# Attention softmax read bank by bank: three maxima and three exponentials in place of one of each

## The reference, cut to what matters

```python
def mla_attend(q_n, q_r, k_n, k_r, v):
    s = jnp.einsum('bqhd,bkhd->bhqk', q_n, k_n) + jnp.einsum('bqhr,bkr->bhqk', q_r, k_r)
    p = jax.nn.softmax(s.astype(jnp.float32) * MLA_SCALE, axis=-1)
    return jnp.einsum('bhqk,bkhd->bqhd', p.astype(v.dtype), v)
```

## Time and profile before

| what | value |
|---|---|
| median of three runs (3574.69 to 3577.97) | 3575.5 us |
| the profiled execution, its own time | 3573.7 us |
| its span from the first to the last instruction | 3570.5 us |
| mean granted TensorE clock | 0.938 |
| PE busy in the span | 3135.9 us, 88% |
| DVE busy in the span | 1529.5 us, 43% |
| ACT busy in the span | 1212.9 us, 34% |

### The profile page before, as it was taken

One profiled execution on the slowest core, in us unless ns is written; L12 is line 12 of the kernel. 1 busy time (PEld: TensorE's weight loads), 2 busy tenths in 40 slices (PEclk: granted clock), 3 DMA queues, 4 the chain that ended last, 5 costly groups with the idle time before them and its releaser, 6 DMA issues. The chain is left out here.

```text
span 3570.5 us, 43051 instructions
## 1 busy us (share of the span) xinstructions
PE 3135.9 (88%) x16797; PEld 2670.6 (75%) x16797; DVE 1529.5 (43%) x2588; ACT 1212.9 (34%) x1951; POOL 147.8 (4%) x146
## 2 busy tenths in 40 slices
PE   4538999999999999995995868789999999999598
PEld 4427898889889988983774646668888888887476
DVE  4352454145325523543232121146656665665333
ACT  2321222223222312322212221146666666665310
POOL 0000000000000000000221000000000000000022
PEclk7768999999999999998997989889999999999899
DMA  5401111111111111115333112100010000000332
GB/s 183 159 1 43 30 35 40 46 32 32 45 36 32 32 51 30 32 32 185 95 100 107 38 44 79 62 25 30 28 31 20 26 28 31 21 28 18 124 118 65
DMA packets 214950, 196.06 MB, mean 55 GB/s; under 512 B 9950, under 2 KB 190574, under 8 KB 214770
## 3 DMA queue, kind: packets, MB, share of 16 engines
q1 hardware_dynamic: 197316, 162.62, 14.8%
q0 software_dynamic: 7056, 25.69, 2.0%
q10 hardware_dynamic: 10400, 5.24, 0.5%
HBM read 152.62 MB, written 40.91 MB: 54 GB/s over the span
## 5 line engine op out<-in xcount | busy, mean ns | idle before, releaser
L40 PE MATMUL v_pj<-e_u_hi,v_w_hi 128*128 128x512 f32 (+1 forms) x1728 | 624.5, 361 | 19.3 <-issue 10.3
L41 PE MATMUL v_pj<-e_u_lo,v_w_hi 128*128 128x512 f32 (+1 forms) x1728 | 620.6, 359 | 0.6 <-issue 0.4
L42 PE MATMUL v_pj<-e_u_hi,v_w_lo 128*128 128x512 f32 (+1 forms) x1728 | 620.4, 359 | 0.0
L40 PEld LDWEIGHTS v_pj<-e_u_hi,v_w_hi 128*128 128x128 f32 x1728 | 329.8, 191 | 67.0 <-issue 20.1
L42 PEld LDWEIGHTS v_pj<-e_u_hi,v_w_lo 128*128 128x128 f32 x1728 | 329.3, 191 | 51.8 <-issue 0.7
L41 PEld LDWEIGHTS v_pj<-e_u_lo,v_w_hi 128*128 128x128 f32 x1728 | 329.9, 191 | 47.1
L40 PE MATMUL o_y_bank<-o_w_hi,o_m_hi 128*128 128x512 f32 x576 | 235.9, 410 | 71.9 <-DVE o_w_lo L1095 69.5
L1592 ACT CAST t_pt_hi<-t_ring 128x512 fp32r<-128x512 f32 (+1 forms) x384 | 181.3, 517 | 252.2 <-PE t_ring L1775 252.2
L40 PE MATMUL l_pj<-l_u_hi,l_w_hi 128*128 128x512 f32 (+3 forms) x376 | 160.8, 428 | 81.8 <-DVE l_w_lo L1323 60.7
L41 PE MATMUL o_y_bank<-o_w_lo,o_m_hi 128*128 128x512 f32 x576 | 231.5, 402 | 0.0
L42 PE MATMUL o_y_bank<-o_w_hi,o_m_lo 128*128 128x512 f32 x576 | 231.0, 401 | 0.0
(11 more groups left out here) (327 smaller groups left out, 6219.6 us busy)
## 6 DMA issues: line engine op xcount, KB each, us to landing
v_w_raw<-in_ev_w_in SPq DMA_DIRECT2D x73, 512.0 KB, 3.8
m_w_raw<-in_mod_w SPq DMA_DIRECT2D x24, 1024.0 KB, 5.7
l_w_raw<-in_od_w_in SPq DMA_DIRECT2D x21, 512.0 KB, 4.0
o_m_raw<-mixT SPq DMA_DIRECT2D x20, 512.0 KB, 3.8
mixT<-v_buf SPq DMA_DIRECT2D x16, 512.0 KB, 2.7
o_w_raw<-in_ev_w_out SPq DMA_DIRECT2D x16, 512.0 KB, 3.4
zgT<-l_lat POOLq DMA_DIRECT2D x16, 512.0 KB, 3.1
t_zg<-zgT SPq DMA_DIRECT2D x32, 256.0 KB, 2.7
```

The costliest lines, as they stand in the source:

```text
L40: nc.tensor.matmul(out, whi, xhi, start=first, stop=False)
L41: nc.tensor.matmul(out, whi, xlo, start=False, stop=False)
L42: return nc.tensor.matmul(out, wlo, xhi, start=False, stop=last)
```

## The change

The row's maximum, the exponentials and their sum are now made per bank of `S`. The matmul that finishes a bank increments `qk_done` (three per slot). DVE takes the maximum of each bank as soon as that bank is done, into one column of the new tile `tops`, and then reduces the three columns to the negated maximum in `bias`, after a wait on its own semaphore `top_ok`. ACT makes three exponentials (512, 512 and 256 columns), each with its own sum in a column of `sums` and its own increment of `exp_ok`. PE waits before each bank for the exponential of that bank of the tile before. DVE adds the three sums into `total`, waits for itself (`total_ok`) and takes the reciprocal. The diff:

```diff
+        tops, sums = ([s.sb(f"{n}{x}", [P, 3]) for x in range(2)] for n in ("tops", "sums"))
...
                 act.wait_ge(bias_ok, tile(h, t) + 1)
-                nc.scalar.activation(prob[x][:, :], S[:, 0:T], ACT.Exp, bias=bias[x][:, :], accum_out=total[x][:, :]).then_inc(exp_ok, 1)
+                for j, (k0, n) in enumerate(KEYS):
+                    nc.scalar.activation(prob[x][:, k0:k0 + n], S[:, k0:k0 + n], ACT.Exp, bias=bias[x][:, :],
+                                         accum_out=sums[x][:, j:j + 1]).then_inc(exp_ok, 1)
...
             def maximum(h, t):
-                dve.wait_ge(qk_done, tile(h, t) + 1)
-                nc.vector.tensor_reduce(bias[t % 2][:, :], S[:, 0:T], AX, ALU.max, negate=True).then_inc(bias_ok, 1)
+                for j, (k0, n) in enumerate(KEYS):
+                    dve.wait_ge(qk_done, 3 * tile(h, t) + j + 1)
+                    nc.vector.reduce_max(tops[t % 2][:, j:j + 1], S[:, k0:k0 + n], axis=AX).then_inc(top_ok, 1)
+                dve.wait_ge(top_ok, 3 * tile(h, t) + 3)
+                nc.vector.tensor_reduce(bias[t % 2][:, :], tops[t % 2][:, :], AX, ALU.max, negate=True).then_inc(bias_ok, 1)
 
             def inverse(h, t):
-                dve.wait_ge(exp_ok, tile(h, t) + 1)
+                dve.wait_ge(exp_ok, 3 * tile(h, t) + 3)
+                nc.vector.tensor_reduce(total[t % 2][:, :], sums[t % 2][:, :], AX, ALU.add).then_inc(total_ok, 1)
+                dve.wait_ge(total_ok, tile(h, t) + 1)
                 nc.vector.reciprocal(rec[t % 2][:, :], total[t % 2][:, :]).then_inc(rec_ok, 1)
...
-                if (h, t) != (0, 0):
-                    pe.wait_ge(exp_ok, tile(h, t))
-                for k0, n in KEYS:
+                for j, (k0, n) in enumerate(KEYS):
+                    if (h, t) != (0, 0):
+                        pe.wait_ge(exp_ok, 3 * tile(h, t) - 2 + j)
                     out = S[:, k0:k0 + n]
...
-                    last = nc.tensor.matmul(out, qs[b][:, tok], kr2[1][:, k0:k0 + n], start=False, stop=True)
-                last.then_inc(qk_done, 1)
+                    nc.tensor.matmul(out, qs[b][:, tok], kr2[1][:, k0:k0 + n], start=False, stop=True).then_inc(qk_done, 1)
```

More of the change, by code:

```diff
@@ L1476, in stage_attend @@
         ring_done, ring_hi, ring_free = s.sem("ring_done"), s.sem("ring_hi"), s.sem("ring_free")
-        qk_done, bias_ok, exp_ok, rec_ok, prob_ok = (s.sem(n) for n in ("qk_done", "bias_ok", "exp_ok", "rec_ok", "prob_ok"))
+        qk_done, top_ok, bias_ok, exp_ok, total_ok, rec_ok, prob_ok = (s.sem(n) for n in (
+            "qk_done", "top_ok", "bias_ok", "exp_ok", "total_ok", "rec_ok", "prob_ok"))
         turn_ok, qs_hi_ok, qs_ok = s.sem("turn_ok"), s.sem("qs_hi_ok"), s.sem("qs_ok")
```

## The result

| what | before | changed |
|---|---|---|
| median | 3575.61 us (4 runs) | 3600.03 us (4 runs, 3598.66 to 3603.65) |
| the profiled execution, its own time | 3573.7 us | 3599.6 us |
| its span | 3570.5 us | 3597.7 us |
| mean granted TensorE clock | 0.938 | 0.937 |
| attention: PE's first to last matmul in the span | 2320.5 to 3336.6 | 2321.2 to 3364.6 |

The changed kernel takes 1.0069 times the time before, 95% interval 1.0051 to 1.0086: 24.4 us more, where 26.6 more were forecast. The attention grew from 1016.1 to 1043.4 us, by 27.3, which is the whole difference of the two spans.

A forecast was written before the change was run, and what follows sets the result against it. PE was taken to set the pace, with the ACT-DVE ring full in weight-split slots; 3.90 us per pair times seven, +1.2 (head 14), -1.9 (head 15) gave +26.6, hence 3602 us, range 3583 to 3622.

The forecast's parts named there:

- What bounds the kernel: Attention stretch: PE busy 933 of 964 us sets the pace; the ring of ACT and DVE has no room in split slots.
- the ring of ACT and DVE: Exponential, sum, normalise, cast, low half, next maximum: 5.67 us per qn turn, 6.27 with splits; the change adds 1.06.
- Prices: Costs per turn: three exponentials +0.51 us, join of the sums +0.20, three maxima with their join +0.35.
- E: Start of a tile's (first) exponential; a turn from E to E was forecast at 6.73 us in qn slots, 7.33 with splits.
- Restart: PE restarts on bank 0 0.83 us after E instead of 1.47, saving 0.64 once per run of slots.
- E does not come earlier: Maximum comes 0.84 us sooner when DVE waits for PE, but ACT's casts hold E to within 0.1.
- The sum: Four runs of two turns per head pair: +0.35, +1.51, +1.19, +0.85, together 3.90 us; whole kernel +26.6.
- Rival 1: Faster: ring grows under 0.6 us per turn, the loop through PE stays the bound; 3555 us, chance 0.07.
- Rival 2: No change: joins at 0.06 us, pieces 0.03 cheaper each, ring grows by 0.7; 3575 to 3582 us, chance 0.09.
- Rival 3: Clearly slower: exponential pieces can't overlap reads of the sums, 0.2 to 0.3 us more per turn; about 3617, chance 0.14.
- Rival 4: No release by bank: waits break PE's stream or late exponentials leave no restart gain; 19 us more, 3621, chance 0.04.
- Signs named: Profile signs: last read 1.9 us after E, normalise 2.36, no DVE idle before maxima, PE's waits up, new waits before PV.

## Why the prediction was right, point by point

**What bounds the kernel.** Right. PE sets the pace where it can, the ring of ACT and DVE elsewhere, and the reading that the latter had no room in slots with splits was the one that decided: there the turn grew by 1.01 and the run by 1.36 (15.34 for 13.98).

**Prices.** The exponentials are 0.688, 0.688 and 0.477, taken as 0.69, 0.69 and 0.477 from a line of layer 0. Their starts stand 0.68 and 0.66 apart, so a piece does overlap the read of the sum before it: the condition of the third rival fails. Maxima 0.683 and 0.415 (taken as 0.69 and 0.42), joins 0.156 (taken as 0.16). Every turn came out 0.05 to 0.09 below the forecast. The steps that were off are small: in a qn turn normalise starts 2.34 after E instead of 2.36, and from the first maximum to the next exponential it is 1.84 (2851.75 to 2853.59) instead of 1.84 + 0.04 = 1.88, mostly because the three maxima occupy 1.61 and not 1.64. In a rotation turn 0.07 of the 0.09 lie ahead of the first operation of the rotation (2.55 after E instead of 2.62): the join of the sums, priced there, is hidden behind ACT's cast.

**Restart.** 0.83 after E forecast, 2829.11 to 2829.94 measured, 0.83.

**E does not come earlier.** Nearly right. E of the first tile of a run comes 4.58 after its scores begin (2842.34 to 2846.92) instead of 4.70 (2824.34 to 2829.04). The casts set it now, as forecast. In the kernel before they did not: E followed the end of the maximum (2829.00), and behind the casts alone it could have come 0.11 sooner. That small amount was won in four runs: 0.44 per pair.

**The sum.** Runs: odd to even 14.14 (14.29 forecast), even to odd 15.34 (15.49), rotations 16.65 (16.85), v to PV 19.51 (19.60). Together 3.31 per pair instead of 3.90, less 0.44 for E, 2.87 in all. Head 15 gained 2.25 instead of 1.9.

**What was missed.** The clock. By the terms alone seven pairs would have come to 20 us and the total to about 19. The trace has 27.3; the 1.58 in six odd heads, 9.5 us, brings the sum to 28, within 1 of it. So the forecast of 26.6 stands so close to the result partly because two misses cancel: turns taken 0.05 to 0.09 too long and an effect not thought of. The step at fault is the one that costs PE's wait in t = 5 of an odd head at its own length alone.

**Rivals.** Rival 1 (ring grows by under 0.6) fell: it grew by 1.0. Its premise was sound, as the version with the ring relieved shows: where the ring is not the later one, the release pays (3553.89, near the 3555 worked out for this rival, though with DVE's work in another order). Rival 2 needed joins of 0.06. Rival 3 fell with the starts 0.68 apart. Rival 4 fell: without the release by bank the kernel is 29 to 32 us slower still. Its price of 0.64 in four runs per pair was one run too many, since the run with v does not end in scores.

**Signs named.** Last read 1.93 after E (2848.62 + 0.23), forecast 1.9; normalise 2.34, forecast 2.36; no idle of DVE between the low half and the maxima; PE's waits up from 63.0 to 84.3; waits of up to 0.7 before the eight PV of even heads. PE's two new waits inside a slot cost nothing that a row shows.

## What to carry to other kernels

Before work is split up so that one engine can restart sooner, find the ring that does not pass through this engine and add up one turn of it, with every small operation and hand-over: 0.38 us of joins per turn, on an engine idle for over half of the time, carried some 21 of the 24 us of the loss. Two changes that each fit into the same slack don't fit together, so costs found one at a time can't be added. And when the ring is the bound, first move work out of it (here behind the next tile's maxima), since only then does the early release pay: alone the two edits cost 24 and 10 us, together they gained 22.

## What the runs showed of the hardware that was not expected

**A single wait can halve the clock behind it.** In the attention PE is busy nearly without a break, and yet the granted clock fell to 1.2 GHz around the restart behind one wait in t = 5 of an odd head, at the earliest 0.2 us before it and at the latest 1.5 us after it, each time for 3.41 us. Over the kernels run, by PE's idle time there:

| kernel | idle before the restart, us | odd heads in which the clock fell |
|---|---|---|
| relieved ring (both versions) | none | 0 of 7 and 0 of 7 |
| before, with the low halves moved | 0.43 | 0 of 7 |
| kn twice (two runs) | 0.8 | 0 of 7 and 0 of 7 |
| before | 1.43 | 0 of 7 |
| three maxima alone | 1.73 | 0 of 7 |
| three exponentials alone | 1.85 to 1.90 | 4 of 7 |
| no joins | 2.0 to 2.16 | 4 of 7 |
| changed (two runs) | 2.18 to 2.23 | 6 of 7 and 6 of 7 |
| PE waits for all three | 2.20 | 5 of 7 |

The wait and the fall go together, and filling the wait with useless matmuls undid the fall. Head 15 fits in: its falls stand behind waits of 1.83 us or more, but most of its waits of that length have none. Why the clock falls only behind some waits of the same length, no run was made to show. The Trainium skill's page "VectorE: DVE Perf Modes" ("Rules for kernel authors"), which speaks for fewer chained operations rather than fewer semaphores, is borne out with a number: 0.156 us for a 128 x 3 join, 0.035 to 0.04 for the wait ahead of it.

**ACT's read of an accumulated sum is nearly free between two activations.** It takes 0.19 to 0.23 us, starts 0.10 before the activation ends, and the next activation starts 0.09 after it (2829.69, 2829.78 in the changed kernel). From E to the end of the last read it is 1.93 us with three pieces (2846.92 to 2848.85) and 1.42 with one, so each further piece costs 0.25 us, the read included.
